# Two chained transformer networks: the first's projection with permuted columns, the second's norms tile by tile

## The reference, cut to what matters

```python
def trunk_layer(x, cx, c, c_ctx, ...):                        # first network
    u = (rmsnorm(x, g_mix) * (1 + sc1) + sh1) @ w_in          # 1024 -> 2080; the same for cx
    p, gq, gk, gv, gg, rf, rb, aq, ak, av = split_in(u)
    mix = concat([pool_mixer(p), gla_output(gla(gq, gk, gv, rf, rb), gg), attention(aq, ak, av)]) @ w_out
    x = x + ga1 * mix
    x = x + ga2 * squared_relu_mlp(rmsnorm(x, g_mlp) * (1 + sc2) + sh2, w_up, w_down)

def second_block(x, ...):                                     # second network, per layer
    h = rmsnorm_2(x, g_mix_pre) * (1.0 + scale_a) + shift_a
    y = hybrid_mixer(h, w_in, ...)                            # h @ w_in is 1024 -> 1956; ends in o @ w_out
    x = x + gate_a * rmsnorm_2(y, g_mix_post)
    h = rmsnorm_2(x, g_ffn_pre) * (1.0 + scale_f) + shift_f
    x = x + gate_f * rmsnorm_2(swiglu(h, w_gate_up, w_down), g_ffn_post)
```

## Time and profile before

| what | us |
|---|---|
| median of 3 runs | 2006.28 (2004.70 to 2008.29) |
| the profiled execution | 2009.39 |
| its span in the profile | 2007.6 |
| TensorE busy | 1788.9 (89%) |
| VectorE busy | 1121.1 (56%) |
| ScalarE busy | 688.0 (34%) |
| GpSimd busy | 96.2 (5%) |

### The profile page before, as it was taken

One profiled execution on the slowest core, in us unless ns is written; L12 is line 12 of the kernel. 1 busy time (PEld: TensorE's weight loads), 2 busy tenths in 40 slices (PEclk: granted clock), 3 DMA queues, 4 the chain that ended last, 5 costly groups with the idle time before them and its releaser, 6 DMA issues.

```text
span 2007.6 us, 25506 instructions
## 1 busy us (share of the span) xinstructions
PE 1788.9 (89%) x10612; PEld 1454.1 (72%) x10612; DVE 1121.1 (56%) x1727; ACT 688.0 (34%) x811; POOL 96.2 (5%) x91
## 2 busy tenths in 40 slices
PE   5998888789999999988879996997899979879997
PEld 2775646677877777775558995775799756759996
DVE  3475454564445445555477675555766565566654
ACT  2323333132222122423334443454333333534331
POOL 1010001110000000010010000000100010010000
PEclk8999877899999999897889998898899989879999
DMA  8324455124333344334754545450555554325642
GB/s 325 124 86 168 169 197 202 42 75 149 133 126 126 129 159 144 105 136 147 257 192 171 203 175 206 151 190 10 161 187 164 180 199 152 126 63 182 196 159 93
DMA packets 172371, 309.20 MB, mean 154 GB/s; under 512 B 3264, under 2 KB 54720, under 8 KB 171616
## 3 DMA queue, kind: packets, MB, share of 16 engines
q1 hardware_dynamic: 168592, 293.98, 42.1%
q10 hardware_dynamic: 3376, 12.02, 1.8%
q0 software_dynamic: 288, 1.57, 0.2%
HBM read 305.46 MB, written 2.10 MB: 153 GB/s over the span
## 4 chain that ended last, share of the span: by engine, by line
PE 69%; DVE 16%; ACT 5%; issue 5%; DMA 3%; POOL 1%; DVEq 0%; ACTq 0%; SPq 0%; POOLq 0%
PE bank L535 53%; PE twin L535 14%; DVE ring_r L1159 4%; DVE arena L1159 3%; PE bank L544 3%; ACT arena L1884 2%; ACT arena_r L1884 2%; DMA ring<-in_w_in 2%; DMA ring<-in_w_mod 2%; POOL rs L2235 1%; DVE params L1159 1%; DVE arena_r L1159 1%; DVE X L1636 1%; DVE params L1622 0%; DVE arena L1249 0%
## 5 line engine op out<-in xcount | busy, mean ns | idle before, releaser
L535 PE MATMUL bank<-arena_r 128*128 128x512 f32 (+3 forms) x2144 | 710.2, 377 | 14.5 <-DVE arena_r L1754 6.7
L1159 DVE TENSOR_TENSOR ring_r<-ring,arena_r 128x4096 fp32r<-128x4096 f32 (+4 forms) x94 | 393.7, 4188 | 233.3 <-ACT arena_r L1884 232.7
L535 PEld LDWEIGHTS bank<-arena_r 128*128 128x128 f32 x2144 | 412.2, 192 | 95.8 <-issue 7.9
L1884 ACT ACTIVATE arena_r<-ring 128x4096 fp32r<-128x4096 f32 (+4 forms) x94 | 323.0, 3436 | 432.9 <-PE bank L535 160.5
L535 PE MATMUL twin<-actT_r,arena_r 128*128 128x256 f32 x1408 | 254.5, 284 | 1.2 <-DVE actT_r L1159 1.2
L535 PE MATMUL bank<-arena_r,actT_r 128*128 128x512 f32 (+4 forms) x640 | 227.1, 386 | 25.7 <-DVE ring_r L1159 14.2
L535 PE MATMUL bank<-ring_r,arena_r 128*128 128x512 f32 x624 | 246.0, 394 | 0.0
L1884 ACT ACTIVATE arena<-bank 128x512 f32<-128x512 f32 (+6 forms) x170 | 85.7, 504 | 426.2 <-PE bank L535 329.8
L535 PEld LDWEIGHTS twin<-actT_r,arena_r 128*128 128x128 f32 x1408 | 219.8, 192 | 2.0 <-DVE actT_r L1159 2.0
L535 PE MATMUL twin<-actT_r,ring_r 128*128 128x256 f32 x704 | 199.2, 283 | 0.0
L535 PE MATMUL bank<-ring_r,actT_r 128*128 128x512 f32 (+4 forms) x512 | 191.7, 374 | 0.0
(11 more groups left out here) (183 smaller groups left out, 1753.0 us busy)
## 6 DMA issues: line engine op xcount, KB each, us to landing
ring<-in_w_mod SPq DMA_DIRECT2D x24, 2048.0 KB, 8.0
ring<-in_w_ada SPq DMA_DIRECT2D x24, 2048.0 KB, 8.2
ring<-in_w_gate_up SPq DMA_DIRECT2D x44, 1024.0 KB, 7.7
ring<-in_w_down SPq DMA_DIRECT2D x20, 2048.0 KB, 7.8
ring<-in_w_up SPq DMA_DIRECT2D x16, 2048.0 KB, 7.8
ring<-in_w_in SPq DMA_DIRECT2D x12, 2048.0 KB, 8.7
ring<-in_w_out SPq DMA_DIRECT2D x8, 2048.0 KB, 11.7
ring<-in_w_down SPq DMA_DIRECT2D x8, 1792.0 KB, 7.5
```

The source lines that it names most:

```text
L535: ins = nc.tensor.matmul(out_, lhsT, rhs, start=start, stop=stop)
L1159: return v.tensor_tensor(o, x, y, op)
L1884: return nc.scalar.activation(o, x, func, **kw)
```

## The change

**One: columns.** `w_in` of the first network is permuted before the launch (`OLD1`), so that its pieces are `AK RF AV` (288), `GK GV` (512), `AQ` (512), `GQ GG` (512), pool (256). In layer 1 the two context tiles skip every piece but the first two: 14 jobs instead of 16. The gate matmuls use the `s` ring, two tiles at a time, and ScalarE does Exp, Exp, Ln, Ln for them. The sums and norms of q and k move to other jobs.

**Two: the second network's norms.** `residual2`, `squares2`, `normed2` and `turned2` go tile by tile: ScalarE squares the `v` banks in place of VectorE's copy and square; tile 0 is added, normed, transposed and modulated before tile 1. VectorE modulates features 0 to 3 and ScalarE 4 to 7 (`high_ready`), each by 128-wide operations; TensorE's first `linear` waits for both (`turned`). The last split ahead of the norm is cut in two, half beside each tile. Between the networks tile 0 is turned ahead of tile 1's final norm.

**Three: a load's place.** In `loads()` the first piece of the second network's projection comes ahead of a modulation load.

```diff
-GQ, GK, GV, GG, RF, AQ, AK, AV = 256, 512, 768, 1024, 1280, 1312, 1824, 1952
-CH1 = [(1024, 1312), (1312, 1824), (1824, 2080), (512, 1024), (0, 512)]
+GK, GV, GQ, GG, PL, AQ, AK, RF, AV = 0, 256, 512, 768, 1024, 1280, 1792, 1920, 1952
+CH1 = [(1792, 2080), (0, 512), (1280, 1792), (512, 1024), (1024, 1280)]
+OLD1 = [(512, 1024), (256, 512), (1024, 1280), (0, 256), (1312, 1952), (1280, 1312), (1952, 2080)]
...
-        out += [("par2a", l, 0)] + take(1) + ins[:3] + [("par2b", l, 0)] + take(1) + ins[3:] + take(2)
+        out += [("par2a", l, 0)] + ins[:1] + take(1) + ins[1:3] + [("par2b", l, 0)] + take(1) + ins[3:] + take(2)
...
-            if l == L - 1 and t >= 2:
-                if c in (1, 4):
-                    continue
-                if c == 0:
-                    lo = RF - c0
+            if l == L - 1 and t >= 2 and c >= 2:
+                continue
...
+def gate_tiles(l, j, behind):
+    n = j - jobs_until(l, 1) - behind
+    return [n, n + 1] if n in (0, 2) else []
...
-                    mark["rT", l] = k["v"]
-                t = j - jobs_until(l, 1) - 1
-                if 0 <= t < 4:
-                    done("v", mark["rT", l])
-                    b, filled = take("v")
+                    mark["rT", l] = k["s"]
+                for t in gate_tiles(l, j, 1):
+                    done("s", mark["rT", l])
+                    b, filled = take("s")
                     mm(b[:, :], rT[:, t * P:(t + 1) * P], par1("wg")[0:33, :], inc=filled)
-                    mark["z", l, t] = k["v"]
+                    mark["z", l, t] = k["s"]
...
+            def linear(out_, lhs, rhs, inc, order=range(KT), turned={}):
                 for i in order:
+                    if i in turned:
+                        pe.wait_ge(act_ready, nth(act_ready, turned[i]))
...
+            def normed2(n):
+                for t in range(TS):
+                    pe.wait_ge(xn_ready, nth(xn_ready))
+                    for g, r in enumerate("va"):
+                        b, filled = take(r)
+                        for i in range(4):
+                            ft = 4 * g + i
+                            tr(b[:, i * P:(i + 1) * P], normal(n)[:, t, ft * P:(ft + 1) * P], filled if i == 3 else None)
...
+            def turned2(t):
+                c = slice(t * P, (t + 1) * P)
+                b = filled()
+                for ft in range(4):
+                    step(v.tensor_scalar(act2_lo[:, ft, c], b[:, ft * P:(ft + 1) * P], modT[:, 1, ft, 0:1],
+                                         modT[:, 0, ft, 0:1], ALU.mult, ALU.add), v_emptied if ft == 3 else v_step)
+                step(v.tensor_copy(actT_r[:, 0:4, c], act2_lo[:, 0:4, c]))
+                rest(act2_lo[:, 0:4, c], act2_lo_r[:, 0:4, c], actT_r[:, 0:4, c], act_ready)
+                dve.wait_ge(high_ready, nth(high_ready))
+                rest(act2_lo[:, 4:8, c], act2_lo_r[:, 4:8, c], actT_r[:, 4:8, c], act_ready)
...
-                t = j - first - 3
-                if 0 <= t < 4:
+                    b = filled("s")
+                    step(v.tensor_copy(rT[0:32, :], b[0:32, :]), s_emptied)
+                for t in gate_tiles(l, j, 3):
                     dve.wait_ge(zlog_ready, nth(zlog_ready))
                     step(tt(la[:, t, :], la[:, t, :], zt[t % 2], ALU.subtract), la_ready if t == 3 else v_step)
-                t = j - first - 1
-                if 0 <= t < 4:
-                    b = filled()
+                for t in gate_tiles(l, j, 1):
+                    b = filled("s")
                     step(v.tensor_scalar(la[:, t, :], b[:, :], 0.0, None, ALU.min))
                     step(v.scalar_tensor_tensor(out=zt[t % 2], in0=la[:, t, :], scalar=2.0, in1=b[:, :],
-                                                op0=ALU.mult, op1=ALU.subtract), v_emptied)
-                t = j - (k_done - len(tiles1(l)))
+                                                op0=ALU.mult, op1=ALU.subtract), s_emptied)
...
+                t = j - jobs_until(l, 2) - 1
...
-                t = j - k_done - 2
-                if 0 <= t < 4:
+                for t in range(4):
+                    if j != k_done + (2 + t if l < L - 1 else min(1 + t, 3)):
+                        continue
                     if t == 0:
                         dve.wait_ge(rstd_ready, nth(rstd_ready))
+                    aq_norm(l, t)
...
+                if t == 1:
+                    turned2(0)
...
-            def residual2(keys, behind):
+            def residual2(keys, late, n):
                 dve.wait_ge(ga_in, nth(ga_in, 32))
+                def scaled(t, half):
+                    c = slice(half * MODC, (half + 1) * MODC)
+                    b = filled()
+                    mean = ms[:, t:t + 1]
+                    dve.wait_ge(gsq_ready, nth(gsq_ready))
+                    if half == 0:
+                        step(v.tensor_scalar(mean, ss[:, t:t + 1], 1.0 / D, EPS, ALU.mult, ALU.add))
+                    else:
+                        v.scalar_tensor_tensor(out=mean, in0=ss[:, 2 + t:3 + t], scalar=1.0 / D, in1=mean,
+                                               op0=ALU.mult, op1=ALU.add).then_inc(ms_ready, 1)
+                        handed.append(("power", t, 1))
+                    step(tt(y2[:, t, c], b[:, :], GA[:, 0, c], ALU.mult), v_emptied)
+                def added(t):
+                    dve.wait_ge(rstd_ready, nth(rstd_ready))
+                    step(v.scalar_tensor_tensor(out=X[:, t, :], in0=y2[:, t, :], scalar=rs[:, t:t + 1],
+                                                in1=X[:, t, :], op0=ALU.mult, op1=ALU.add), x_ready)
                 for half in range(2):
                     c = slice(half * MODC, (half + 1) * MODC)
                     for key in keys[half]:
-                        split(after(key))
+                        if key != keys[1][-1]:
+                            split(after(key))
                         if key == keys[half][0]:
                             gate(0, half)
                             step(tt(GA[:, 0, c], GA[:, 0, c], post[:, c], ALU.mult))
                     for t in range(TS):
-                        b = filled()
-                        y = y2[:, t, c]
-                        step(v.tensor_copy(y, b[:, :]), v_emptied)
-                        squares(junk2, y, t)
-                        mean = ms[:, t:t + 1]
-                        if half == 0:
-                            step(v.tensor_scalar(mean, ss[:, t:t + 1], 1.0 / D, EPS, ALU.mult, ALU.add))
-                            step(tt(y, y, GA[:, 0, c], ALU.mult))
-                        else:
-                            v.scalar_tensor_tensor(out=mean, in0=ss[:, t:t + 1], scalar=1.0 / D, in1=mean,
-                                                   op0=ALU.mult, op1=ALU.add).then_inc(ms_ready, 1)
-                            handed.append(("power", t, 1))
-                            step(tt(y, y, GA[:, 0, c], ALU.mult))
-                for t in range(TS):
-                    dve.wait_ge(rstd_ready, nth(rstd_ready))
-                    step(v.scalar_tensor_tensor(out=X[:, t, :], in0=y2[:, t, :], scalar=rs[:, t:t + 1],
-                                                in1=X[:, t, :], op0=ALU.mult, op1=ALU.add), x_ready)
-                for t in range(TS):
-                    behind(t)
+                        if half and late:
+                            split_part(late, t, False)
+                        scaled(t, half)
+                        if half:
+                            added(t)
+                            if n and t == 1:
+                                turned2(0)
+                            if n:
+                                norm_tile(t, n)
+                if n:
+                    turned2(1)
...
+            def squares2(l, stage, half):
+                n = mark["y", l, 2 * stage + half] - 2
+                for t in range(TS):
+                    act.wait_ge(v_filled, n + t + 1)
+                    step(f(junk2, VB[(n + t) % 2][:, :], ACT.Square, accum_out=ss[:, 2 * half + t:2 * half + t + 1]),
+                         gsq_ready)
+            def normed2(n):
+                for t in range(TS):
+                    squared([t], n)
+                    if t == 0:
+                        act.wait_ge(modT_ready, nth(modT_ready))
+                    c = slice(t * P, (t + 1) * P)
+                    b = filled()
+                    for i in range(4):
+                        step(f(act2_lo[:, 4 + i, c], b[:, i * P:(i + 1) * P], ACT.Identity, scale=modT[:, 1, 4 + i, 0:1],
+                               bias=modT[:, 0, 4 + i, 0:1]), a_emptied if i == 3 else a_step)
+                    step(f(actT_r[:, 4:8, c], act2_lo[:, 4:8, c], ACT.Copy), high_ready)
...
-                t = j - jobs_until(l, 1) - 2
-                if 0 <= t < 4:
-                    act.wait_ge(v_emptied, mark["z", l, t])
+                tiles = gate_tiles(l, j, 2)
+                for t in tiles:
```

(2 more changed lines are left out.)

64 lines of the change are left out of this document (34 added, 30 removed).

## The result

The changed kernel takes 2023.12 us (median, 2019.67 to 2025.02) for 2007.28 us before (2004.70 to 2009.31): a ratio of 1.0081, 95% interval 1.0063 to 1.0100, from four executions of each. That is 15.8 us slower where +12 was forecast, 2018 with a range of 2004 to 2027. The profiled execution took 2023.06 us, its span is 2021.0, with a mean granted clock of 0.909 for 0.917 before.

The account below looks back on a forecast made before the run. TensorE was taken as the bound wherever operands are there, its waits for VectorE's normed tile the largest. Terms 9.6 + 4.6 + 0.9 + 1 - 0.6 - 1.5 + 1.7 - 3 = +12.7, taken as +12: 2018 us, range 2004 to 2027.

Parts of the forecast that it names:

- Output to up projection, twice +4.8: Second network, output to up projection: first tanh 23.9 us after TensorE's end against 20.1, plus 1 of clock; +9.6 for both.
- Rival (a): Output stages: the tile pipeline hides the norms, each stage gaining about 2 us; 1998 us, chance 0.13.
- The load, +4.6 in layer 0: Second network's projection: the third piece waits for the first piece's slot, so its split and matmuls come later; +4.6 us.
- Between the networks, +0.9: Between the networks: turning tile 0 ahead of tile 1's chain puts the first matmul at 1262.2 for 1261.34; +0.9 us.
- the layer's end: Down projection to next layer's projection: earlier load gains 4.1 us, then the third piece's wait spends it and 1 more; +1.
- Rival (b): Second network's projection: the ring's later load is hidden because that piece is not last there; 2013 us, chance 0.1.
- The end, -1.5: Kernel's end: the last tile's copy and square become one ScalarE square, the first tile's addition leaves the tail; -1.5 us.
- Layer 0's projection of the first network, +1.7: There, the wider third piece holds VectorE's split, gates wait 7.3 for 0.91, the 5.03 wait goes, 0.4 of clock; +1.7 us.
- Layer 1, -3: First network's projection, layer 1: POOL's power released earlier, TensorE resumes 3.9 us sooner, 0.9 given back by idling; -3 us.
- rival (c): First network's projection: batching relieves ScalarE, the 5.03 and most of the 5.59 waits go; 2011 us, chance 0.1.
- rival (d): Output stages and projection: stalls multiply, with the low clock throughout; +20, 2026 us, chance 0.12.
- 0.6: Middle of each down projection: VectorE frees the second bank sooner, -0.3 us each, -0.6 in all.

Follow-up runs that it names:

- whole_split: The changed kernel with the last split ahead of a norm whole again, ahead of tile 0's sum: 1.0060 of the kernel before, stretches 15.99 and 15.86 us.
- load_only: The kernel before with only the second network's first projection piece loaded ahead of the modulation load: ratio 1.0001, no change.
- together_load: together plus load_only's edit, the first piece loaded ahead of the modulation: 0.9955 of the kernel before, no different from together.
- together: The kernel before with bank squares on ScalarE and each tile added once its power is there, both tiles normed and turned together: ratio 0.9950.
- cols_norms: The changed kernel with the loads in the order of before: ratio 1.0073 to the kernel before, +14.7 us.
- cols_only: The kernel before with only the first network's edits (permuted columns, gates in pairs, moved sums): ratio 1.0014, +2.8 us.
- gates_first: cols_only with VectorE's low-half split of the third piece behind its copy of the gate columns: 0.9952 of the kernel before, 9.8 us faster.
- norms_load: The changed kernel without the first network's edits: ratio 1.0055 to the kernel before, +11.0 us.

## Why the prediction was right, and where it was not

**Output to up projection, twice +4.8: right in mechanism, a little small.** The first up matmul was counted 18.2 us behind TensorE's end; it came after 17.84 in both layers, 5.0 and 5.2 later than before. The term itself ends at the first tanh, at 23.9 and 1 of clock; that came after 26.0 and 25.7, so the term measures +5.9 and +5.6. What was too small is the clock: the matmuls up to the tanh were counted at 6.7 with it and took 8.2 and 7.9. Rival (a), the pipeline hiding the norms, fell for the reason named: ScalarE's list has tile 1's bank square first. The count had VectorE held by that square too; the runs add that even with it ahead (14.67) and with the turning moved (14.75) the pipeline loses to the kernel before (12.8). VectorE's list has more behind TensorE's end: the half split, four 128-wide operations for each tile, and all the subtractions, of which GpSimd had done four. That this is the 1.9 us is the reading left over: whole_split moved only the first of the three, and the other two were not tried.

**The load, +4.6 in layer 0: right for the load alone, undersized in the changed kernel.** The stretch of that projection grew by 4.2 in load_only and by 4.6 in together_load against together, but by 7.1 in the changed kernel (72.8 to 79.8), and by 6.6 in layer 1. The mechanism is as told: the third piece is issued when the first is read, and TensorE idles (5.87 us, where some 8 were foretold). Why the tile-wise norms add to it no run isolates.

**Between the networks, +0.9: wrong, in sign and size.** It fell by 7.6. This is the step that failed: I let VectorE's chain start at TensorE's end, as if nothing else held it, and counted only what the turned tile 0 adds. The chain in fact began behind the split of the first piece, at 1237.67, and that split waited for its load, which was issued behind the modulation's. The moved load frees it: load_only alone has 14.4 for 21.8. Whether putting that split later in VectorE's list would do the same without the projection's price was not tried. For the layer's end I had counted the earlier load, and there the first matmul came 4.7 us sooner where 4.1 was forecast. What the tiles do between the networks is nothing: 23.6 in cols_norms and 23.6 in cols_only. So the terms of these stages, +4.6, +0.9 and +1, are +6.5 in all, where the load alone is no change (load_only) and the four stretches of the two traces add up to +1.4: 5 to 6 us too many in my sum. Rival (b) named the right size of the load for the wrong reason: the later load isn't hidden, it is paid for elsewhere.

**The end, -1.5: right,** -1.9 (9.4 to 7.5).

**Layer 0's projection of the first network, +1.7: +3.3** (+3.2 with the columns alone). The wait was forecast at 7.3 and is 7.44, and the 5.03 went. The clock term was mis-sized: 0.4 for 3.4 measured by gates_first, part of which the kernel before paid too, behind its stall of 5.03.

**Layer 1, -3: right,** resumption 2.9 us earlier against the stage's start (895.10 for 892.02, with 6.0 of delay brought along from 796.06 and 802.04); TensorE's idle time there grew to 14.96 as forecast. At the heads, counted from the same start, 2.5 us of it are left.

**The table loads:** eight became four in layer 0, at 1283 ns each in both kernels, and the stage became no faster: rival (c) fell, as the list that held the gates was VectorE's. The Trainium skill (ScalarE: Activation LUTs, What ACT_TABLE_LOAD costs) has 2.66 us for a switch, made up of about 1283 ns for the load and 1380 ns of a drain. The rows agree with the first figure; the second doesn't show in them, as in that projection the next activation starts directly behind each load. Once VectorE's list no longer holds the gates, the columns do gain; how much of that is the batching was not tried.

**The clock, rival (d):** its 2026 is nearer to the 2023 measured than my 2018 is, but a low clock throughout was not what came. The low clock stood behind single stalls: it cost 3.4 us at the gates of layer 0, and the matmuls behind the two output stages take 0.9 and 0.4 us longer than before.

**The sum** was +12.7, with the load's stages too high by 5 to 6 and others too low: the columns by 4 (2.8 measured for -1.3) and the norms by 3 to 4 (10.8 to 11.8 measured for 9.6 - 0.6 - 1.5 = 7.5).

Part of what is missing from the norms can be placed. Up to the first up matmul the stretches give 10.2 less 1.9, 8.3. Up to the first tanh they give 11.5 less 1.9, 9.6, in cols_norms against cols_only. In norms_load against load_only they give 11.8 less 1.9, and the layer's end costs 2.2 more (12.9 for 10.7), 12.1 in all. The rest lies within the intervals.

Of the columns' 4 us, 1.6 stand in layer 0 and some in layer 1. The stretch between the networks is also longer with them: 22.6 to 23.6 in the four kernels with the new columns and the old load order, 21.8 in the two without. I didn't look for its cause. Two slips in the working are small: 1274 + 8.1 + 3.7 is 1285.8 and not 1286.1, and 873.8 + 14.5 is 888.3 and not 888.1.

That the forecast came near, +12 for +15.8, is partly luck, as these errors had opposite signs.

## What to carry to other kernels

By these runs a pipeline over tiles pays only where the engine that ends last has idle time between the tiles; add up its list from the producer's end, and if the list only grows, work on the whole at once and take copies off that engine instead. Where an engine takes splits and copies in one list, ask of each copy what it stands behind: a small copy behind a split whose load lands late cost more here than all that the new column order gained. And before costing an interval by the chain one means to change, read what its first instruction was waiting for.

## What the runs showed of the hardware

Four gate matmuls behind 7.25 us of idle TensorE took 3.78 us, and 1.98 without the wait. The windows of the two kernels (us, busy time by engine with counts, granted clock, DMA share, GB/s), cols_only and then gates_first:

```profile
85.03:88.81 3.78, 3.78 (x5) 1.24 (x5) 1.38 (x2) 0.09 (x1) 0.00 (x0) 0.50 0.00 0
88.81:101.50 12.69, 12.69 (x49) 10.10 (x49) 3.46 (x5) 3.71 (x5) 0.00 (x0) 0.87 0.00 0
```

```profile
77.96:79.94 1.98, 1.98 (x6) 0.74 (x5) 1.20 (x1) 1.27 (x2) 0.00 (x0) 1.00 0.83 304
79.94:91.00 11.06, 11.06 (x49) 8.89 (x49) 8.06 (x8) 3.81 (x5) 0.00 (x0) 1.00 0.00 0
```

The granted clock was 0.50 there (1.2 GHz) and 1.00 (2.4 GHz) without the wait, and the low clock reached into the next 48 matmuls. So this stall cost half as much again as its length, which a sum of waits doesn't hold.

Instructions that no edit touches don't take the same time in each profile: from the heads of layer 0 to those of layer 1 the kernel before took 740.0 us and load_only, with the same instructions there, 732.5; eight matmuls near the start took 4.50 in one and 7.19 in the kernel after. A single span can't be read to better than that. Short stretches made of waits agree better between kernels that share them: the one from output to up projection was 17.84 or 17.85 six times, and 12.5 to 12.8 in the eight cases of kernels that leave it as it was.
